# Two units' rests in one VectorE instruction of 2048 columns, in a decoder block with split weights

## The reference

```python
xn = rmsnorm(h, norm_w[l], NORM_EPS)
proj = xn @ w_in[l]                      # 2048 x 18432
(rq, rk, rv, rz, dq, dk, dv, dz, g_ret, g_diff) = jnp.split(proj, SPLIT_POINTS, axis=-1)
...
o_ret = retention(rq, rk, rv)            # 8 heads, rotated q and k, chunks of 128
o_ret = rmsnorm(o_ret, None, NORM_EPS).reshape(b, s, RET_WIDTH) * jax.nn.silu(rz)
...
o_diff = diff_attention(dq, dk, dv, lam) # 8 heads, two softmaxes, one minus lam times the other
o_diff = rmsnorm(o_diff, subln_w[l], SUBLN_EPS) * (1.0 - lam_init)
o_diff = o_diff.reshape(b, s, DIFF_WIDTH) * jax.nn.silu(dz)

mixed = (jax.nn.sigmoid(g_ret) * (o_ret @ w_ret_up[l])
         + jax.nn.sigmoid(g_diff) * (o_diff @ w_diff_up[l]))
h = h + mixed @ w_out[l]
return rmsnorm(h, final_norm_w, NORM_EPS)
```

## Time and profile before

| | before |
|---|---|
| time, median of 3 runs | 1080.47 us (1079.97 to 1080.58) |
| the profiled execution's own time | 1081.05 us |
| its span, first to last instruction | 1079.2 us |
| PE busy | 1069.4 us, 4834 matmuls |
| DVE busy | 818.0 us, 1026 instructions |
| ACT busy | 561.4 us, 716 instructions |
| granted TensorE clock, mean | 0.998 |
| HBM read | 210.84 MB, 197 GB/s over the span |

### The profile page before, as it was taken

The page is one execution under the profiler, slowest core; times in us unless marked ns, Lnnn a source line. Parts: engine busy times, 40 slices in busy tenths (PEclk is TensorE's granted clock), DMA queues, the critical chain, the costliest instruction groups (busy, mean ns, idle before and its releaser), DMA issues.

```text
span 1079.2 us, 13347 instructions
## 1 busy us (share of the span) xinstructions
PE 1069.4 (99%) x4834; PEld 889.3 (82%) x4834; DVE 818.0 (76%) x1026; ACT 561.4 (52%) x716; POOL 55.6 (5%) x89
## 2 busy tenths in 40 slices
PE   9999999999999999999999999999999999999997
PEld 7888888888888888888888888888888888888875
DVE  6687876865888978867768687787869875677876
ACT  6555464545545544434644644564465554445454
POOL 0100000000000000000100020010002000111100
PEclk9999999999999999999999999999999999999999
DMA  9886666766665565767576667767766666765753
GB/s 323 302 258 191 235 190 201 226 184 194 179 213 198 190 222 171 223 183 242 167 224 200 202 204 210 222 197 202 214 191 183 217 214 238 233 229 194 271 198 117
DMA packets 120162, 227.98 MB, mean 211 GB/s; under 512 B 14496, under 2 KB 36768, under 8 KB 119584
## 3 DMA queue, kind: packets, MB, share of 16 engines
q1 hardware_dynamic: 118784, 224.76, 66.1%
q0 software_dynamic: 1024, 2.10, 0.6%
q10 hardware_dynamic: 288, 0.27, 0.1%
HBM read 210.84 MB, written 2.10 MB: 197 GB/s over the span
## 4 chain that ended last, share of the span: by engine, by line
PE 97%; DVE 1%; DMA 1%; issue 1%; ACT 0%; DVEq 0%; POOLq 0%; POOL 0%; SPq 0%; ACTq 0%
PE bank L1684 20%; PE bank L1686 20%; PE bank L1685 20%; PE bank L1691 11%; PE bank L1692 11%; PE bank L1693 11%; PE bank L1763 1%; PE bank L1762 1%; PE bank L1761 1%; PE bank L1656 0%; DMA raw<-w_out_dram 0%; PE bank L1660 0%; PE bank L1663 0%; PE bank L1821 0%; DMA raw<-w_in_dram 0%
## 5 line engine op out<-in xcount | busy, mean ns | idle before, releaser
L821 ACT ACTIVATE w_hi<-raw 128x1024 fp32r<-128x1024 f32 x344 | 362.5, 1059 | 404.2 <-PE bank L1686 284.1
L1180 DVE TENSOR_TENSOR w_lo<-raw,w_hi 128x1024 fp32r<-128x1024 f32 x344 | 421.6, 1236 | 197.6 <-ACT w_hi L821 196.6
L1684 PE MATMUL bank<-w_hi,xt_hi 128*128 128x512 f32 x816 | 318.9, 391 | 0.0
L1686 PE MATMUL bank<-w_hi,xt_lo 128*128 128x512 f32 x816 | 317.7, 389 | 0.0
L1685 PE MATMUL bank<-w_lo,xt_hi 128*128 128x512 f32 x816 | 317.5, 389 | 0.0
L1686 PEld LDWEIGHTS bank<-w_hi,xt_lo 128*128 128x128 f32 x816 | 153.2, 188 | 32.2
L1685 PEld LDWEIGHTS bank<-w_lo,xt_hi 128*128 128x128 f32 x816 | 153.2, 188 | 31.4
L1684 PEld LDWEIGHTS bank<-w_hi,xt_hi 128*128 128x128 f32 x816 | 153.2, 188 | 31.4 <-DVE w_lo L1180 0.3
L1691 PE MATMUL bank<-w_hi,xt_hi 128*128 128x512 f32 x364 | 141.7, 389 | 1.1 <-issue 1.1
L1692 PE MATMUL bank<-w_lo,xt_hi 128*128 128x512 f32 x364 | 141.6, 389 | 0.0
L1693 PE MATMUL bank<-w_hi,xt_lo 128*128 128x512 f32 x364 | 141.6, 389 | 0.0
(11 more groups left out here) (211 smaller groups left out, 1089.6 us busy)
## 6 DMA issues: line engine op xcount, KB each, us to landing
raw<-w_in_dram SPq DMA_DIRECT2D x284, 512.0 KB, 4.3
raw<-w_ret_up_dram SPq DMA_DIRECT2D x32, 512.0 KB, 4.7
raw<-w_diff_up_dram SPq DMA_DIRECT2D x32, 512.0 KB, 4.6
raw<-w_out_dram SPq DMA_DIRECT2D x32, 512.0 KB, 4.5
rot<-squares_t SPq DMA_DIRECT2D x64, 64.0 KB, 2.2
zs<-squares_t SPq DMA_DIRECT2D x48, 64.0 KB, 2.2
normed<-squares_t SPq DMA_DIRECT2D x48, 64.0 KB, 2.2
raw<-w_in_dram SPq DMA_DIRECT2D x8, 256.0 KB, 6.0
```

Of the source, the lines that this page charges most:

```text
L821: act.activation(w_hi[:, s, :, :], raw[:, s, :, :], ACT.Copy).then_inc(hi_ready, 1)
L1180: dve.tensor_tensor(w_lo[:, s, :, :], raw[:, s, :, :], w_hi[:, s, :, :].bitcast(F32), ALU.subtract) \
L1684: pe.matmul(bank[bk][:, :], hi, w_hi[:, s, kk, :], start=k == 0, stop=False)
L1686: return pe.matmul(bank[bk][:, :], lo, w_hi[:, s, kk, :], start=False, stop=k == KT - 1)
```

## The change

DVE takes the rests of two plain units n, n+1 (n even) in one instruction over both ring slots, 2048 columns. It stands where unit n+1's rest stood, waits for `hi_ready` to count n+1, and raises `units_split` by 4 at its end. Where unit n's rest stood there is nothing. This holds from unit 28 on, except in sevens. 160 pairs replace 320 of the 344 instructions of L1180; 24 single ones stay at the start. The third and fourth load of x move from behind units U_OUT+17 and U_OUT+18 (369, 370) to behind U_OUT+13 and U_OUT+14 (365, 366).

```diff
-X_AGAIN_AT = (U_TAIL + 20, U_TAIL + 28, U_OUT + 17, U_OUT + 18)
+X_AGAIN_AT = (U_TAIL + 20, U_TAIL + 28, U_OUT + 13, U_OUT + 14)
...
+def in_seven(n):
+
+    group, k = paired(n)
+    return group is not None and k // KU in SEVEN_AT
+
+
+def rests_together(n):
+
+    return n >= len(ORDER) + RING and not in_seven(n)
...
-                dve.wait_ge(hi_ready, n + 1)
-                dve.tensor_tensor(w_lo[:, s, :, :], raw[:, s, :, :], w_hi[:, s, :, :].bitcast(F32), ALU.subtract) \
-                   .then_inc(units_split, 2)
+                if rests_together(n) and n % 2:
+                    dve.wait_ge(hi_ready, n + 1)
+                    dve.tensor_tensor(w_lo[:, s - 1:s + 1, :, :], raw[:, s - 1:s + 1, :, :],
+                                      w_hi[:, s - 1:s + 1, :, :].bitcast(F32), ALU.subtract).then_inc(units_split, 4)
+                elif not rests_together(n):
+                    dve.wait_ge(hi_ready, n + 1)
+                    dve.tensor_tensor(w_lo[:, s, :, :], raw[:, s, :, :], w_hi[:, s, :, :].bitcast(F32), ALU.subtract) \
+                       .then_inc(units_split, 2)
                 if behind is not None and not sums_first(n):
                     rest_of_sums(group, behind)
```

## The result

The change makes the kernel slower: 1183.0 us (median of 4 runs, 1182.3 to 1184.2) against 1080.51 us, a ratio of 1.0953 with a 95% interval of [1.094, 1.0967]. The forecast was 1156 us with a range of 1136 to 1174: the right sign, but too little. The profiled execution has a span of 1181.6 us, 102.4 more than before.

The account below looks back on a forecast made before the run. PE, busy 99% of the span, was taken as the bound. Waits of 58.5 us and 17 us for the clock on 1081.05 us gave 1156.6, stated as 1156 us against the median; range 1136 to 1174.

Parts of the forecast that it names:

- term 1: At 13 of the 18 sevens PE waits 3.04 us each for the common rest behind: 39.5 us.
- term 2: Sevens 100 and 292, where the rest of the sums comes later: waits of 1.81 us, 3.6 us for two.
- term 3: Sevens 106 and 298, with reads of the heads' outputs in between: waits of 4.22 us, 8.4 us for two.
- term 4: At seven 378, unit 383 is rounded late, so PE waits 1.58 us at unit 382.
- term 6: Four rotations in a row in the second retention iteration: 0.9 us of waits.
- DVE's saving: 160 pairs save 0.18 us each, 29 us of DVE's busy time, worth nothing with PE at 99% busy.
- I price plain pairs at nothing: At plain pairs the common rest ends 1.8 us before PE wants it, so no wait: 0 us.
- term 5: Rotations in differential attention, two places in each of four iterations: 8 waits of 0.71 us, 5.7 us.
- the clock: Long waits at 15 sevens lower PE's granted clock in two of three: 10 falls of 1.7 us, 17 us.
- small waits: Small waits left out of the terms; some 2 us for them was put into the forecast's own range.
- The second rival: The clock falls at every long wait and stays low as long as at the start: 1176 us, chance 0.05.

Follow-up runs that it names:

- experiment 2: The change, but the two units behind each of the 18 sevens keep single rests in their old places: 1107.38 us.
- experiment 3: The change with common rests only for the 18 pairs behind sevens, all else single as in the kernel before: 1154.28 us.
- experiment 5: The change, but at the common rest's place two single rests of 1024 columns, each releasing its own unit: 1132.59 us.
- experiment 7: Kernel before with the x loads moved; only PE waits for both units' rests before it begins the even one: 1121.81 us.
- experiment 10: Kernel before with the x loads moved and 24 common rests, away from sevens and rotations: 1079.7 us.
- Experiment 9: The change with single rests behind sevens and for 8 units from the first rotation on in each differential iteration: 1097.49 us.
- Experiment 6: Kernel before with the x loads moved; only SP waits for both rests of a pair before loading the even unit's successor: 1083.11 us.
- experiment 4: The change, but a seven's rest of the sums is taken behind the common rest of units n+2 and n+3: 1151.76 us.

## Why the prediction was too low

**Right: the mechanism and its place.** The common rest behind a seven starts where unit n+3's rest started, and PE waits for its end. 2.9 to 3.0 us were measured at nine of the 13 sevens of term 1, forecast 3.04; terms 2, 3, 4 and 6 are off by 0.4 us at most. Experiments 2 and 3 show the place, 5 and 7 show that it is the common release, which costs about as much as the late place of unit n's rest. DVE's saving was worth nothing, as forecast (experiment 10).

**Wrong: "I price plain pairs at nothing", as far as their loads are concerned.** This is the step that failed, and it made terms 1 and 5 too small by 9 us together. I checked a load against ACT only in an undisturbed pair: issued at 3.65 us, landed at 7.95, wanted at 8.36. That is 0.4 us of cover, not the 1.8 of PE's side. It is gone wherever ACT wants the load sooner after the common rest, the load lands later, or side work delays the common rest.

- *Behind the first seven of a group.* Unit n+2 of a seven loads when the common rest of n-2 and n-1 ends. At seven 116 this rest ends at 344.04 and ACT wants unit 118 at 347.80, 3.8 us later and not 4.7 as in the undisturbed pair (8.36 - 3.65). The load landed after 3.5 us, so ACT still waited for PE:

```profile
347.80 1.07 ACT L832 ACTIVATE w_hi<-raw 128x1024 fp32r<-128x1024 f32 x1 [1.17 <-PE bank L1709]
```

  At seven 132 the common rest of 130 and 131 ends at 396.11; unit 134's load leaves then and lands 4.4 us later. ACT's rows in the changed kernel:

```profile
400.65 1.06 ACT L832 ACTIVATE w_hi<-raw 128x1024 fp32r<-128x1024 f32 x1 [2.48 <-DMA raw<-w_ret_up_dram]
401.61 1.90 ACT L785 ACTIVATE v_hi<-zs 128x2048 fp32r<-128x2048 f32 x1
```

  Unit 134 is rounded late, behind it the sums, behind them their rest and then the common rest: the wait is 4.18 us where it is 2.88 in experiment 3, in which 130 and 131 have single rests. Of these 1.3 us some 0.5 come from the common rest, which is later against the seven than at 116 (DVE waited for ACT there, which rounded 131 behind a tile of side work), and 0.9 from the load, which takes 4.4 us and not 3.5; 0.2 were spare. The same happens at 150 (4.32), 358 (4.56) and 374 (3.57). At 374 the common rest is no later than at 116 (at both it ends 1.1 us before ACT rounds the seven), so the load's 4.3 us are the whole cause:

```profile
1134.43 1.06 ACT L832 ACTIVATE w_hi<-raw 128x1024 fp32r<-128x1024 f32 x1 [1.26 <-DMA raw<-w_out_dram]
```

  The first sevens of the groups at 32, 112 and 304, whose loads landed in 3.5 to 3.8 us, wait 2.88. So what sets the four apart is the landing time of their loads (weights of the retention up-projection and the output projection) at least as much as the side work. Why these loads take longer is open; no experiment separates the two. Together the four make the 3.7 us that term 1 was short, less what the others fell below 3.04.

- *At the second rotation.* The wait was forecast at 0.71 and is 1.9 to 2.2 us. I hadn't counted the turning DMAs, which stand in SP's queue between the loads. SP's and ACT's rows in the changed kernel, behind the first rotation:

```profile
535.99 0.37 SPq L598 DMA_DIRECT2D raw<-w_in_dram  x1
536.41 2.50 SPq L606 DMA_DIRECT2D normed<-squares_t  x4
538.95 1.11 SPq L598 DMA_DIRECT2D raw<-w_in_dram  x2
```

```profile
540.11 1.06 ACT L832 ACTIVATE w_hi<-raw 128x1024 fp32r<-128x1024 f32 x1 [2.99 <-DMA raw<-w_in_dram]
...
543.28 1.06 ACT L832 ACTIVATE w_hi<-raw 128x1024 fp32r<-128x1024 f32 x1 [1.59 <-DMA raw<-w_in_dram]
```

  Unit 178's load leaves at the common rest's end, 535.97; four turning DMAs follow with 2.5 us of issuing, and unit 179's load leaves at 538.95. It lands 4.3 us later, so 179 is rounded only at 543.28, the rotation starts late, and so does the common rest behind it. Experiment 9 takes this cause away, and the second wait shrinks to the forecast's size in three iterations of four. Experiment 6 shows that loads by pairs alone cost under 3 us: they cost what they do because the rests are late as well. The second waits are 5.4 of the 7.3 us that term 5 was short. The other 2.0 stand in the last iteration, where PE waits 1.92 us before unit 270 and 0.78 before 274; their cause is open.

**Mis-sized: the clock.** Forecast 10 falls of 1.7 us, measured 13 spells with 25.6 us lost. The price of a fall was about right in experiment 3 (1.6 to 1.7 us); the number was too small, since 13 of the 15 waits of 2.9 us or more brought one and not two in three. In the changed kernel two of the 13 spells are twice as long as the others, which makes 2.0 us a fall.

**Not priced: small waits** of some 0.5 us at units 192, 224, 256, 288, 336 and 356 and 1.1 at 352, and gaps still smaller. I had put 2 us for them into the range; they are some 8.

**The sum.** 1156 is short by 27: 3.7 of it is term 1, 7.3 term 5, 8 small waits and gaps, 8.6 the clock. The range ended at 1174 because it let only the clock vary, and took the waits as certain. The second rival, with its 1176 us, had the clock heavier than measured and the waits lighter.

## What to carry to other kernels

- Joining two steps of a pipeline delays the first one's release to the second one's end. Look for the place with the least work between the two on the consumer (here 9 matmuls, 2.04 us), not at the average. An instruction that is 0.18 us cheaper cost 3.0 us there.
- A slot that is freed later has two customers: the consumer of the result, and the load that refills it. Check the second one at the places where the engine is already late, with everything that stands in the same DMA queue, and with the landing time of the loads at that place and not the median of all.
- When PE's waits get past some 2 us, price the clock as well: here it added a third to the waits' cost.

## What the runs showed of the hardware

**The granted clock fell at short waits.** In experiment 3 PE waited 2.9 to 4.2 us at 15 sevens and 1.7 us at two. The clock fell 14 times, each time at one of the long waits (ten times in its last 0.5 us, four times 0.8 to 1.5 us after its end), and not at the short ones. In the traces of experiments 3, 4, 5 and 7 no fall came with a wait of 1.9 us or less. Between 2.2 and 3.1 us both outcomes occurred: in experiment 4 the waits of 2.3 us before units 108 and 124 brought one, the waits of 2.5 us before 358 and 3.0 before 374 didn't. The Trainium skill ("TensorE: Matmul & The Clock Gate", why this matters for your kernels) warns of gaps between bursts of matmuls that are somewhat longer than the shortest one here. These runs saw falls at waits of 2.2 and 2.3 us already, and here the measurement decides.

**At 0.50 of the clock matmuls start at half the rate.** In experiment 3, behind the wait at seven 132, they start 0.43 us apart, where 0.23 is regular.

**A load of the same size lands sooner in one stage than in another.** In the changed kernel the 512 KB of unit 118 took 3.5 us from issue to landing, those of unit 134 took 4.4. Units 150, 358 and 374 (4.3 to 4.4 us) are like the latter, 38 and 310 (3.5 to 3.8) like the former. The cause is open.
